# First block's output projection on one Trainium2 core: plain matmuls against four column pairs in seven products each

## The reference

```python
a_out = pool_mixer(u, pool_w[i], pool_scale[i])
b_out = chunk_attention(q, k, v, rel_bias[i])
mix = jnp.concatenate([a_out, b_out], axis=-1) @ mix_w_out[i]     # 512x1024 @ 1024x1024
...
x = x + gate1[:, None, :] * mix
h2 = modulate(rmsnorm(x, norm2_w[layer]), shift2, scale2)
ffn = hier_moe(h2, moe_w_group[layer], ...)                       # 32 experts, two per row
```

## Time and profile before

| | |
|---|---|
| time, median of 3 runs | 3481.84 us (3480.09 to 3485.37) |
| profiled execution, its own time | 3490.99 us |
| profiled execution, span in the trace | 3488.8 us |
| PE busy | 3280.4 us, 94% of the span |
| output projection with its modulation parts, in the trace | 235.57 to 299.60 us |
| share of that stretch in the span | 64.03 us, 1.8% |

### The profile page before, as it was taken

One profiled execution on the slowest core, in us unless ns is written; L12 is line 12 of the kernel. 1 busy time (PEld: TensorE's weight loads), 2 busy tenths in 40 slices (PEclk: granted clock), 3 DMA queues, 4 the chain that ended last, 5 costly groups with the idle time before them and its releaser, 6 DMA issues.

```text
span 3488.8 us, 36853 instructions
## 1 busy us (share of the span) xinstructions
PE 3280.4 (94%) x13528; PEld 2083.5 (60%) x13528; DVE 1788.1 (51%) x3350; ACT 906.9 (26%) x1864; POOL 288.1 (8%) x246
## 2 busy tenths in 40 slices
PE   8988989999998989988999999999989899999997
PEld 4743544777744545555555555555544566778886
DVE  2343236777713337787334454444468854554454
ACT  2231212344312221144232131111112523222222
POOL 1200421333101320000000000000000000000000
PEclk9988999999998999999999999999999999999998
DMA  8746876533355971101111212212222021222331
GB/s 270 230 137 200 342 276 206 175 90 92 115 181 204 363 266 53 37 13 41 37 49 37 61 43 57 64 55 56 65 61 61 19 65 49 65 69 81 89 85 61
DMA packets 418495, 394.01 MB, mean 113 GB/s; under 512 B 27888, under 2 KB 353648, under 8 KB 410896
## 3 DMA queue, kind: packets, MB, share of 16 engines
q1 hardware_dynamic: 384768, 348.01, 31.5%
q10 hardware_dynamic: 15120, 23.68, 2.2%
q0 software_dynamic: 18432, 19.98, 1.7%
HBM read 440.78 MB, written 31.52 MB: 135 GB/s over the span
## 4 chain that ended last, share of the span: by engine, by line
PE 61%; DVE 5%; ACT 3%; DMA 2%; issue 1%; DVEq 0%; ACTq 0%; POOL 0%; POOLq 0%
PE psum L714 38%; PE psum L699 6%; PE psum L1198 3%; PE psum L912 2%; DVE arena L2131 2%; PE psum L1284 2%; PE psum L1332 2%; ACT arena L1569 2%; DMA ring<-in_w_branch 1%; PE psum L931 1%; PE psum L1352 1%; PE psum L1364 1%; DVE arena L2128 1%; ACT arena L1561 1%; PE psum L897 1%
## 5 line engine op out<-in xcount | busy, mean ns | idle before, releaser
L714 PE MATMUL psum<-arena,ring 128*128 128x384 f32 (+1 forms) x2592 | 748.3, 439 | 12.9 <-DVE arena L2128 5.3
L714 PEld LDWEIGHTS psum<-arena,ring 128*128 128x128 f32 x2592 | 493.0, 191 | 238.9 <-DVE psum L2128 11.2
L714 PE MATMUL psum<-hT,ring 128*128 128x384 f32 (+1 forms) x2176 | 624.6, 440 | 1.9 <-ACT part_sum L1569 1.9
L714 PEld LDWEIGHTS psum<-hT,ring 128*128 128x128 f32 x2176 | 414.6, 191 | 192.1 <-issue 8.1
L1569 ACT ACTIVATE part_sum<-psum 128x256 f32<-128x256 f32 (+1 forms) x408 | 174.2, 429 | 953.5 <-PE psum L714 809.2
L2128 DVE TENSOR_TENSOR psum<-psum,part_sum 128x256 f32<-128x256 f32 (+1 forms) x328 | 156.1, 480 | 386.3 <-PE psum L714 277.5
L2128 DVE TENSOR_TENSOR ring<-ring 128x512 f32<-128x512 f32 (+1 forms) x336 | 215.9, 662 | 261.2 <-PE psum L714 258.4
L1569 ACT ACTIVATE arena<-psum 128x256 f32<-128x256 f32 (+5 forms) x501 | 210.3, 465 | 505.2 <-PE psum L699 187.9
L699 PE MATMUL psum<-hT,ring 128*128 128x512 f32 (+1 forms) x832 | 313.8, 539 | 16.8 <-DVE hT L2124 14.5
L1561 ACT ACTIVATE arena<-psum,cols 128x256 f32<-128x256 f32 (+3 forms) x280 | 131.7, 493 | 632.2 <-PE psum L912 190.7
L699 PEld LDWEIGHTS psum<-hT,ring 128*128 128x128 f32 x832 | 160.5, 194 | 170.0 <-issue 157.5
(11 more groups left out here) (252 smaller groups left out, 3699.1 us busy)
## 6 DMA issues: line engine op xcount, KB each, us to landing
ring<-in_w_in SPq DMA_DIRECT2D x172, 512.0 KB, 4.1
arena<-in_moe_w SPq DMA_DIRECT2D x44, 1536.0 KB
ring<-in_ada_w SPq DMA_DIRECT2D x96, 512.0 KB, 6.1
ring<-in_w_mod SPq DMA_DIRECT2D x48, 512.0 KB, 5.9
ring<-in_ssm_w_in SPq DMA_DIRECT2D x48, 512.0 KB, 5.5
ring<-in_w_branch SPq DMA_DIRECT2D x64, 256.0 KB, 3.1
hT<-in_moe_w SPq DMA_DIRECT2D x10, 1536.0 KB
ring<-in_moe_w SPq DMA_DIRECT2D x10, 1024.0 KB
```

The lines of the kernel that those rows point to most:

```text
L714: mm = nc.tensor.matmul(flat(bank_, nb), lhs[:, k, :], rhs(k), start=(start and k == 0), stop=(k == kd_ - 1), skip_group_check=True)
```

## The change

The output projection goes through the same pair functions, with the letter "O": four pairs of column blocks, each with a modulation part `quad_part(3, i)` ahead of its tail. POOL makes the weight sums behind those of `inA`, DVE makes T1 to T4 out of `aT`. `quad_turn(3)` moves behind the first modulation part of the next stage. SP's loads follow the new order, and experts 2 and 3 now wait for the end of block 1.

```diff
             for k in range(4):
                 eng.wait_ge(vector_done, pe.at(("aoutA", k)))
-            for h in range(8):
-                eng.wait_ge(scalar_done, pe.at(("oA_c", h)))
-            for c in range(8):
-                if c % 2 == 0:
-                    quad_part(3, c // 2)
-                linear(("outA", c), lambda k: aT[:, k, :])
-                if c == 6:
-                    quad_turn(3)
+            st["kept"] = True
+            for i in range(4):
+                pair_head("O", i)
+                pair_middle("O", i, lambda: quad_part(3, i))
+                pair_tail("O", i)
+            st["kept"] = False
             if stage_on(2):
                 quad_part(QUAD_MOE[0], 0)
+                quad_turn(3)
                 norm_sum("n2_0")
                 moe(0)
...
                     elif e == 2:
-                        eng.wait_ge(tensor_done, sp.at(("full",) + jobname("out" + "AM"[l], 0, "x")))
+                        eng.wait_ge(tensor_done, sp.at(("full",) + jobname("out" + "AM"[l], 1 - l, "x")))
...
             for c in range(8):
                 if c in (2, 4):
                     expert_put(0, c - 2, c - 1)
-                if c % 2 == 0:
+                put(block8(a["mix_w_out"][0], P * c))
+                if c % 2:
                     quad_put(3, c // 2)
-                put(block8(a["mix_w_out"][0], P * c))
...
+            at_half = lambda k0, h: aT[:, k0:k0 + 4, S // 2 * h:S // 2 * h + S // 2]
+            tt(T_out[0], at_half(0, 1), at_half(0, 0), ALU.subtract).then_inc(vector_done, ve.step(("T1", "O")))
+            for h in range(8):
+                eng.wait_ge(scalar_done, ve.at(("oA_c", h)))
+            eng.wait_ge(vector_done, ve.own())
+            tt(T_out[1], at_half(4, 1), T_out[0], ALU.subtract).then_inc(vector_done, ve.step(("T2", "O")))
+            tt(at_half(0, 1), at_half(4, 1), at_half(0, 1), ALU.subtract).then_inc(vector_done, ve.step(("T3", "O")))
+            eng.wait_ge(vector_done, ve.own())
+            tt(T_out[2], at_half(4, 0), T_out[1], ALU.subtract).then_inc(vector_done, ve.step(("T4", "O")))
+            for p in range(4):
+                c11("O", p)
+                c12("O", p)
+                c22("O", p)
+                for k in (2 * p, 2 * p + 1):
+                    b, free = full("outA", k, "x")
+                    stt(xT[:, k, :], b, M(0, 2, k), xT[:, k, :], ALU.mult, ALU.add).then_inc(vector_done, ve.step([free, ("xA", k)]))
                     if k:
-                        sum_square(norm, k - 1)
-                sum_square(norm, KD - 1)
+                        sum_square("n2_0", k - 1)
+            sum_square("n2_0", KD - 1)
...
             for i in range(1, 8):
                 pair_sums("A", i)
+            for i in range(4):
+                pair_sums("O", i)
```

More of the change, by code:

```diff
@@ L337, in program @@
         inA_sums = [mH.take(12, P) for _ in range(2)]
+        mO = Arena(at=aT.shape[1] * S, end=2 * aT.shape[1] * S)
+        out_sums = [mO.take(12, P) for _ in range(2)]
+        T_out_4 = mO.take(4, S // 2)
+        T_out = Arena(at=mA.at, end=MODW - 2 * EW).take(2, 4, S // 2)
+        T_out = [T_out[:, 0], T_out[:, 1], T_out_4]
         mE = Arena()
@@ L421, in pair_jobs @@
                 return jobname("inA", 2 * n, "x"), jobname("inA", 2 * n + 1, "x")
+            if g == "O":
+                return jobname("outA", 2 * n, "x"), jobname("outA", 2 * n + 1, "x")
             return tuple(jobname("ssm", g, c, "x") for c in SSM_PAIRS[n])
         def pair_before(g, n, back=1):
+            if g == "O":
+                return ("O", n - back) if n >= back else ("A", 7) if back == 1 else None
             m = n - 1 - back if g == "A" else 3 * g + n - 3 - back
@@ L995, in pair_head @@
                 x = job(*b_[1:])
-                half_product(x[0], wa[0][:, 0:4, :], low(0), True, ("Q1", g, n))
+                half_product(x[0], wa[0][:, 0:4, :], low(g, 0), True, ("Q1", g, n))
                 w = job(*a_[1:])
-                half_product(w[0], wa[0][:, 4:8, :], high(0), True, ("Q2", g, n))
+                if (g, n) == ("O", 0):
+                    for h in range(8):
+                        eng.wait_ge(scalar_done, pe.at(("oA_c", h)))
+                half_product(w[0], wa[0][:, 4:8, :], high(g, 0), True, ("Q2", g, n))
                 two[g, n] = wa, wb, x
             def pair_middle(g, n, beside=None):
-                sums, st_ = pair_sum_tile(g, n), "A" if g == "A" else "ssm"
+                sums, st_ = pair_sum_tile(g, n), kind_of(g)
                 wa, wb, x = two[g, n]
@@ L1018, in pair_middle @@
                 eng.wait_ge(vector_done, pe.at(("T3", st_)))
-                half_product(x[0], wb[0][:, 0:4, :], low(1), False, ("Q7", g, n))
+                half_product(x[0], wb[0][:, 0:4, :], low(g, 1), False, ("Q7", g, n))
                 if beside:
@@ L1728, in _ @@
                 router_load(0)
-                squares("n2_0", lambda k: xT[:, k, :], lambda k: (quad_out(3) if k == 6 else None, eng.wait_ge(vector_done, ac.at(("xA", k)))))
+                for p in range(4):
+                    part_copy("O", p, 1)
+                    part_copy("O", p, 3)
+                    part_copy("O", p, 2)
+                    if p == 3:
+                        quad_out(3)
+                    squares("n2_0", lambda k: xT[:, k, :], lambda k: eng.wait_ge(vector_done, ac.at(("xA", k))), n=2, first=2 * p)
                 inv_root("n2_0", D, col("eps"), ahead=True)
@@ L3229, in pair_sums @@
                 wa, wb = ring[:, slot[0]], ring[:, slot[1]]
+                if (g, n) == ("O", 0):
+                    eng.wait_ge(tensor_done, po.at(("full",) + jobname("scA", 7, 3)))
                 used = pair_before(g, n, 2)
```

21 lines of the change are left out of this document (10 added, 11 removed).

## The result

The median went from 3485.37 us (7 runs, 3479.48 to 3488.85; the three shown ahead are among them) to 3496.24 (7 runs, 3491.90 to 3499.36). The medians are 10.9 us apart. The ratio on record is 1.0037, interval 1.0025 to 1.0049, or some 13 us (9 to 17). That is slower, as forecast, but +6.3 was the forecast, and 3496.24 is outside its range, which ended at 3494. Read from the start of the second-last head's output matmul (226.80 in the earlier trace rows, 225.07 after), the norm's sum comes at 302.20 - 226.80 = 75.40 before and at 313.67 - 225.07 = 88.60 after, +13.2 us. The traces put the slowdown into this stretch, 2.5% of the span of after.

A forecast was written before the change was run, and what follows sets the result against it. PE's unbroken work was taken to bound the kernel. Savings of 8.8 us against load waits of 5.5 and 5.6 and 4.0 for the clock gave +6.3, a median of 3488.1 us, range 3479 to 3494.

The forecast's parts named there:

- What goes away: Output projection up to the norm's sum: PE time saved by the pair form and covered idle time, 8.8 us.
- What is added off the path: POOL's 16 weight sums, partly during the last attention heads, and DVE's T1 to T4: covered, taken as 0.
- Rival (d): Pairs 2 and 3: POOL's sums serial with PE, 2 x 1.3 us at most; chance 0.17 together with the low-clock rival.
- The first new wait: Ahead of pair 2: PE waits 5.5 us for blocks 4 and 5, loaded behind modulation loads and experts; bounds 3.9 to 5.9.
- The second new wait: Modulation part behind the last tail: PE waits 5.6 us for loads into ring slots that this tail frees.
- What the waits do to the clock: Behind the two new waits: PE falls to the lower clock, 2.0 us each, 4.0 in all, ends 0 and 5.1.
- Rival (c): Router's matmuls: the clock stays low into them, some 4 us over six steps, 3492 us; chance 0.17 with the POOL-sums rival.
- The sum: Whole kernel: -8.8 + 5.5 + 5.6 + 4.0 = +6.3 us, median from 3481.84 to 3488.1 us.

The follow-up runs named there:

- e7_pool_alone: The kernel before, plus eight unused POOL sums of 128x512 right after the last attention scores; nothing else changed. Ratio 1.0021.
- e1_pool_late: The changed kernel, with the weight sums of the first two pairs started only after DVE has scaled the last head. Ratio 1.0017.
- e2_experts_apart: The changed kernel, with expert 2 loaded behind the weights of blocks 4 and 5, expert 3 behind those of 6 and 7. Ratio 1.0011.
- e3_last_plain: The changed kernel, with blocks 6 and 7 as plain blocks, the last modulation part between them and loads in that order. Ratio 1.0018.
- e6_part_behind_norm: The changed kernel, with the next stage's modulation part 0 behind the norm's sum, part 1 behind the router's first step, part 3 behind the logits. Ratio 1.0023.
- e4_three_edits: The changed kernel with late weight sums, blocks 6 and 7 plain, and experts 2 and 3 loaded apart. Ratio 0.9977 to the kernel before.
- e5_four_pairs_clean: The changed kernel with four pairs, late weight sums, experts 2 and 3 apart, next stage's modulation parts moved behind norm's sum and logits. Ratio 0.9983 to the kernel before.
- e0_before_again: The kernel before, run once more with no line changed. Ratio 0.9992, interval 0.9982 to 1.0002.
- e11_pool_alone_later: The kernel before, plus eight unused POOL sums of 128x512 started after DVE has scaled the last head. Ratio 1.0000.

## Why the forecast was off

**What goes away** was right. Pairs 1 and 3 take 14.1 us from tail to tail, modulation part included (264.71 - 250.58 = 14.13, 302.18 - 288.04 = 14.14), as in the earlier trace rows.

**What is added off the path** is the step that failed. It took POOL's 16 sums at 0, since their weights and buffers are there and POOL is idle. It looked for what the sums meet among T1 to T4 alone. But the stretch that it named, "during the last attention heads", holds DVE's four scalings of the last head, and the head's transposes, output matmul and the whole projection stand behind them. They went from 1.28 to 5.27 us, and the matmul behind fell to the lower clock: +5.7 us where 0 was taken, reproduced without the rest of the change by `e7_pool_alone` (+6.2) and removed by `e1_pool_late` (-5.9). It is most of the 6.9 us by which the forecast fell short at the norm's sum (13.2 against 6.3). The operation that meets the sums is a scaling with one tensor operand, which the prediction did not suspect; the Trainium skill (SBUF — State Buffer, two separate sides) names DVE operations in a two-port mode beside those with two SBUF inputs, and the prediction had quoted only the latter. No row tells in which mode a scaling ran. Rival (d), with the sums serial to PE in pairs 2 and 3, was priced at 2.6 us and at another place; in the traces no wait of PE in the pairs is for POOL.

**The first new wait** was right in mechanism and place: `e2_experts_apart` removes it by the order of SP's loads alone. Its size was forecast at 5.5 and measured at 6.6 start to start (6.44 in the row). The stream ran at 346 GB/s over the whole of 252.6:273.1, where 372 was taken behind the first load: the slow start is within it, and so are loads of the next pair, which SP issued from 266.74 on and beside which 306 GB/s were moved. 5.9 at 364 (by the same working rather 5.8) was the upper bound, so the bound was too narrow. The 358 GB/s of the Trainium skill (DMA: Bandwidth & Descriptors, Where 436 GB/s comes from) gave 6.1, nearer than the sum's value. As a bound the trace does not bear it out: in 260.0:266.7 the transfers ran at 427 GB/s.

**The second new wait** was right, 5.6 forecast and 5.34 in the row. `e3_last_plain` removes it by freeing a slot earlier.

**What the waits do to the clock** came out at 2.6 + 1.4 = 4.0 as forecast, though not 2.0 each. The repeats show that it was partly luck: behind a wait of 5.49 us in `e2_experts_apart` the slow stretch lasted into the norm's work. The Trainium skill (TensorE: Matmul & The Clock Gate, Loop structure matters more than you think) says that a long wait for a transfer between matmuls lets the array go to the slow level, and the traces agree: behind each wait of 5.3 us or more in this stretch the next group of matmuls ran at half speed (a part of 1.92 us took 3.24 to 3.64). One of 1.81 us in `e6_part_behind_norm`, shortly behind another of 1.74, was followed by it too; those of 1.41 to 1.87 in `e4_three_edits` were not. Rival (c), a low clock into the router, came for a short while and cost little. PEclk was 0.50 in 319.20:322.60, with the router's matmuls from 319.65 on, but 1.00 in 325:328, and they took 8.49 us against 8.17, where (c) took 4 us for six steps.

**The sum.** -8.8 + 6.6 + 5.5 + 4.0 = +7.3, against 7.5 measured for the projection, and 7.5 with the 5.7 of the last head is the +13.2. The range ended at 3494; on its base of 3481.84 the 13.2 us would have been 3495.0. The base itself was low, 3485.37 over seven runs, which is no error of the mechanism. The first expert matmul moved by 13.5 us, so the delay was carried on as forecast; in the trace some 5 us of it are no longer there at the span's end (+8.1), though the time rose by 11 (medians) to 13 (ratio).

**What stays open.** Local savings do not account for all of the ratios. `e4_three_edits` is 2.6 us ahead at the norm's sum and at the first expert matmul, while its ratio says 8; `e5_four_pairs_clean` is 1.8 ahead there and says 6. Some 3 us may be the scatter that `e0_before_again` shows, and the clock among the attention heads ahead of the stretch differs between executions. The window 183:193 of the kernel before and of `e4_three_edits`:

```profile
183.00:193.00 10.00, 9.08 (x21) 4.84 (x22) 4.45 (x13) 4.47 (x13) 0.00 (x0) 0.50 0.08 25
```

```profile
183.00:193.00 10.00, 8.79 (x41) 4.94 (x39) 7.67 (x22) 5.58 (x17) 0.00 (x0) 1.00 0.09 25
```

The second-last head's matmul starts at 226.80 in the one and at 220.87 in the other, in a part of the program that no edit touches; after, at 0.50 in that window as well, has 225.07. The mean granted clock of the whole execution differs as well: 0.979 in the profiled execution of `e4_three_edits`, against 0.974 and 0.975 in those of the kernel before, and over all runs 0.976 (11) against 0.975 (32). So part of what `e4_three_edits` gains by its ratio goes with a higher clock elsewhere in the program. Whether the edits have a part in that, and that this scatter accounts for the rest of the ratios, is argued, not shown; no run here holds that clock fixed.

## What to carry to other kernels

Work moved to an idle engine isn't free because the engine is: look in the trace at what the engines that it can hold up do in that stretch (here DVE), and above all at short operations with a chain behind them. Here the same sums, started 5.5 us later, cost nothing. When an order of computing frees buffers in bursts, write down which load waits at the head of the queue and what stands behind it, for the load that is wanted first may be behind megabytes that are not. A gain of a few microseconds on PE is worth little until its waits are short: here each wait of 5.3 us or more was paid again in the clock, with 1.4 to 2.6 us in after.

## What the runs showed of the hardware that was not expected

- DVE's `tensor_scalar` of 128x128 to 128x512 (0.29 to 0.48 us alone, in `e11_pool_alone_later`) got through one to each of POOL's `tensor_tensor` of 128x512 (1.27 us): the four took 5.27 us in the changed kernel and 5.19 in `e7_pool_alone`. So a short DVE operation pays for a long POOL operation each time, while POOL's sums beside them kept their 1.26 us (228.26 and 229.60 above). With DVE operations of two tensors in SBUF both sides paid, in `e1_pool_late`: a sum that met T1 took 2.21 us instead of 1.27, and T2 to T4 took 1.92 us each instead of 1.22.
- DVE's adds of 128x256 with one operand in PSUM kept their 0.43 us beside POOL's sums, in `e1_pool_late`:

```profile
233.38 0.42 DVE L2148 TENSOR_TENSOR psum<-psum,part_sum 128x256 f32<-128x256 f32 x1
235.70 0.43 DVE L2148 TENSOR_TENSOR psum<-psum,part_sum 128x256 f32<-128x256 f32 x1 [1.89 <-PE psum L993]
```

- The clock fell also without a wait of several microseconds. In the changed kernel four gaps of 0.51 to 1.03 us between groups of one to four transposes, and one of 0.88 behind them, went with PEclk 0.51 in 230.40:237.30.
